# Projections on TensorE: the three products of a tile for two PSUM banks in turn

## What is computed

```python
def first_block(x, ...):
    h = rmsnorm(x, norm_mix_g)
    rq, rk, rv, rg, dq, dk, dv = split(h @ w_in)          # seven projections of 512 columns
    ret = silu(rg) * rmsnorm(retention(rq, rk, rv))        # 4 heads
    dif = rmsnorm(diff_attention(dq, dk, dv, lam)) * ...   # 4 heads, two softmaxes each
    x = x + concat(ret, dif) @ w_out
    xn = rmsnorm(x, norm_ffn_g)
    return rmsnorm(x + peer(xn, wq, subkeys, u, v))        # 16384 one-neuron experts, top 16 of 8 heads

def second_block(x, ...):
    h = rms_norm(x, norm_g)
    q, k, v, qi, ki, wi, z_a, u_b, z_b, gates = split(h @ w_in_2)
    a = dsa_attention(q, k, v, qi, ki, wi, k_sel) * silu(z_a)   # index scores choose 128 keys
    b = multiscale_pool(u_b, ...) * silu(z_b)
    g = sigmoid(gates + merge_bias)
    y = g[0] * (a @ w_branch_a) + g[1] * (b @ w_branch_b)
    return x + y @ w_out_2
```

## Time and profile before

| | |
|---|---|
| median of 3 executions | 1982.58 us (1982.3 to 1982.94) |
| profiled execution, first to last instruction (span) | 1979.5 us |
| median less the span (start and end around it) | 3.1 us |
| granted TensorE clock, mean | 1.000 |
| PE busy | 1954.4 us, 99% |
| DVE, ACT, POOL busy | 1212.9, 728.8, 875.7 us |

### The profile page before, as it was taken

The page is one execution under the profiler, slowest core; times in us unless marked ns, Lnnn a source line. Parts: engine busy times, 40 slices in busy tenths (PEclk is TensorE's granted clock), DMA queues, the critical chain, the costliest instruction groups (busy, mean ns, idle before and its releaser), DMA issues.

```text
span 1979.5 us, 23758 instructions
## 1 busy us (share of the span) xinstructions
PE 1954.4 (99%) x9127; PEld 1586.5 (80%) x9127; DVE 1212.9 (61%) x2188; ACT 728.8 (37%) x1057; POOL 875.7 (44%) x595
## 2 busy tenths in 40 slices
PE   8999999999999999999999999999999999999999
PEld 6777888888888766888888878888888888787787
DVE  3455442499999774222223588888888874795344
ACT  4345432232333344222223333333333334635452
POOL 1000000006878888887700677777787600720000
DMA  7543333146666667866657799999999923332122
GB/s 245 169 136 121 124 111 127 43 142 146 147 147 144 139 118 199 244 146 146 148 183 253 249 373 355 381 373 349 363 375 359 387 75 96 86 88 62 44 95 85
DMA packets 178592, 374.91 MB, mean 189 GB/s; under 512 B 56880, under 2 KB 92208, under 8 KB 169008
## 3 DMA queue, kind: packets, MB, share of 16 engines
q1 hardware_dynamic: 109264, 277.03, 41.0%
q0 software_dynamic: 64000, 84.12, 16.5%
q10 hardware_dynamic: 5216, 12.26, 1.7%
HBM read 312.38 MB, written 60.95 MB: 189 GB/s over the span
## 4 chain that ended last, share of the span: by engine, by line
PE 95%; DVE 3%; ACT 1%; issue 1%; DMA 0%; SPq 0%; DVEq 0%; ACTq 0%
PE bank L1558 35%; PE bank L329 18%; PE bank L331 17%; PE bank L330 17%; PE bank L1438 1%; PE bank L2237 1%; PE bank L1184 1%; PE bank L2217 1%; PE bank L548 1%; PE bank L2226 1%; PE bank L569 0%; DVE mix L919 0%; PE bank L419 0%; DVE v_low L1813 0%; PE bank L604 0%
## 5 line engine op out<-in xcount | busy, mean ns | idle before, releaser
L1412 POOL DMA_INDIRECT gates_scratch<-slot_gate,slot_place x256 | 441.5, 1725 | 299.4 <-DVE slot_place L1379 205.6
L1558 PE MATMUL bank<-xn_low,u_high 128*128 128x512 f32 x1024 | 410.3, 401 | 0.0
L1558 PE MATMUL bank<-xn_high,u_high 128*128 128x512 f32 x1024 | 399.9, 391 | 0.0
L1558 PE MATMUL bank<-xn_high,u_low 128*128 128x512 f32 x1024 | 398.6, 389 | 0.0
L1609 DVE TENSOR_TENSOR u_low<-u_raw,u_high 128x1024 fp32r<-128x1024 f32 x128 | 156.4, 1223 | 265.1 <-ACT u_high L1580 264.7
L329 PE MATMUL bank<-v_high,w_high 128*128 128x512 f32 x768 | 299.3, 390 | 1.4 <-DVE v_low L1813 1.4
L330 PE MATMUL bank<-v_low,w_high 128*128 128x512 f32 x768 | 299.1, 390 | 0.0
L331 PE MATMUL bank<-v_high,w_low 128*128 128x512 f32 x768 | 299.1, 389 | 0.0
L322 DVE TENSOR_TENSOR weights_low<-weights_raw,weights_high 128x1024 fp32r<-128x1024 f32 (+1 forms) x105 | 127.7, 1217 | 228.2 <-ACT weights_high L311 228.2
L1704 POOL DMA_INDIRECT row_unit<-units_scratch,slot_place x128 | 175.1, 1368 | 145.8 <-DMA units_scratch<-hidden 107.1
L1697 POOL DMA_INDIRECT row<-in_peer_v,row_places x128 | 188.7, 1474 | 82.4 <-DVE x L1824 48.9
(11 more groups left out here) (344 smaller groups left out, 3046.7 us busy)
## 6 DMA issues: line engine op xcount, KB each, us to landing
u_raw<-in_peer_u SPq DMA_DIRECT2D x128, 512.0 KB, 4.1
v_raw<-in_peer_v SPq DMA_DIRECT2D x64, 1024.0 KB, 7.6
weights_raw<-in_w_in SPq DMA_DIRECT2D x62, 512.0 KB, 3.6
hidden_scratch<-hidden SPq DMA_DIRECT2D x128, 192.0 KB
hidden_in<-hidden_scratch SPq DMA_DIRECT2D x32, 768.0 KB, 11.7
gates_scratch<-nothing POOLq DMA_DIRECT2D x32, 512.0 KB, 2.9
gate_in<-gates_scratch SPq DMA_DIRECT2D x32, 512.0 KB, 7.3
weights_raw<-in_w_out SPq DMA_DIRECT2D x16, 512.0 KB, 3.7
```

The lines of the kernel that those rows point to most:

```text
L1412: pool.engine.indirect_dma_start(gates, bass.IndirectOffsetOnAxis(p.slot_place[t][:, i:i + 1], 0), p.slot_gate[t][:, i:i + 1], None, compu ...
L1558: step = pe.engine.matmul(m.bank[b][:, :], left[:, k, :], right[:, k, :], start=(done == 0), stop=(done == 3 * KT - 1))
```

## The change

A new helper issues the first product for two banks, then the second for both, then the third for both. `project_tensor` takes the banks in pairs: it waits for both to be empty, goes over the chunk's tiles with both, signals `multiplied` twice, on the last matmul of either bank, and calls `between()` twice behind the pair. The programs of ACT and DVE are the same as before.

```diff
--- before.py
+++ after.py
@@ -331,6 +331,15 @@
     return engine.matmul(out, ll, rh, start=False, stop=last)
 
 
+def two_banks(engine, items, first, last):
+
+    for out, (lh, ll), (rh, rl) in items:
+        engine.matmul(out, lh, rh, start=first, stop=False)
+    for out, (lh, ll), (rh, rl) in items:
+        engine.matmul(out, lh, rl, start=False, stop=False)
+    return [engine.matmul(out, ll, rh, start=False, stop=last) for out, (lh, ll), (rh, rl) in items]
+
+
 def project_tensor(m, name, data, data_ready, banks, freed, between=None):
 
     st, pe, s = m.stream, m.pe, m.s
@@ -339,25 +348,32 @@
     for c in range(g.chunk, g.end):
         weight_high, weight_low = st.part(st.high[c % st.PAIRS], c), st.part(st.low[c % st.PAIRS], c)
         pe.wait_ge(s.weights_low, c + 1)
-        for i, b in enumerate(banks):
+        for first_bank in range(0, len(banks), 2):
+            two = [(i, banks[i]) for i in range(first_bank, first_bank + 2)]
             if c == g.chunk:
-                m.await_bank(b)
+                for i, b in two:
+                    m.await_bank(b)
             for r in range(g.rows):
                 k = (c - g.chunk) * g.rows + r
-                if i == 0:
+                if first_bank == 0:
                     pe.wait_ge(*data_ready(k))
-                part = slice(i * P, i * P + P if g.token_major else min(i * P + P, g.width))
-                if g.token_major:
-                    left = (high[:, k, part], low[:, k, part])
-                    right = (weight_high[:, r, 0:g.width], weight_low[:, r, 0:g.width])
-                    out = m.bank[b][:, 0:g.width]
-                else:
-                    left = (weight_high[:, r, part], weight_low[:, r, part])
-                    right = (high[:, k, :], low[:, k, :])
-                    out = m.bank[b][0:part.stop - part.start, :]
-                done = three_products(pe.engine, out, left, right, k == 0, k == g.tiles - 1)
-            done.then_inc(s.multiplied, 1)
+                items = []
+                for i, b in two:
+                    part = slice(i * P, i * P + P if g.token_major else min(i * P + P, g.width))
+                    if g.token_major:
+                        left = (high[:, k, part], low[:, k, part])
+                        right = (weight_high[:, r, 0:g.width], weight_low[:, r, 0:g.width])
+                        out = m.bank[b][:, 0:g.width]
+                    else:
+                        left = (weight_high[:, r, part], weight_low[:, r, part])
+                        right = (high[:, k, :], low[:, k, :])
+                        out = m.bank[b][0:part.stop - part.start, :]
+                    items.append((out, left, right))
+                done = two_banks(pe.engine, items, k == 0, k == g.tiles - 1)
+            for step in done:
+                step.then_inc(s.multiplied, 1)
             if between is not None:
+                between()
                 between()
     for i, b in enumerate(banks):
         m.bank_freed[b] = freed(i)
```

## The result

| | before | after |
|---|---|---|
| median | 1982.44 us (1980.76 to 1982.94, 4 executions) | 1996.05 us (1994.42 to 1998.2, 4 executions) |
| ratio | | 1.0072, 95% interval 1.0060 to 1.0084 |
| profiled execution, own time / span | 1980.76 / 1979.5 us | 1998.2 / 1996.9 us |
| granted clock, mean of the execution | 1.000 | 0.995 |

The kernel is slower by 0.7%, 13.6 us. That lies above the forecast of 1986.3 us and above its range. The two profiled executions stand further apart than the medians, 17.4 us: the one of before is the fastest of its four and the one of after the slowest.

What follows compares the result with a forecast made beforehand. TensorE was taken to bound the kernel, busy 1954.4 of 1979.5 us. Losses of 7.8 less gains of 3.9 gave +3.9, taken as +3.7 on 1982.58: 1986.3 us, range 1981.5 to 1990.5.

Steps and rivals of the forecast that it cites:

- item 4: Second block's attention (gate01, gate10, start of gate11): merged transposes and multiplies wait on ACT's copies; 3.2 lost, 1.4 gained, +1.8 us.
- The rival that the lost cover costs much more: Each of 12 pairs of merged pieces stalls about 1 us; 1995 us, or 1989 for half; chance 0.22.
- Rate: Projection matmuls: alternating banks gains nothing, 227 ns either way; wq0 to wq3 should still take 86.5 us.
- the rival of faster alternation: Projections: a fixed 11 ns a matmul is a same-bank cost that falls away, 28 us; 1958 us; chance 0.05.
- Two completion signals: Rival, 210 pairs of bank ends: signals on neighbouring matmuls cost time, 2 us at 0.01 us each; 1988 us; chance 0.05.
- Item 1: ret_gate: ACT and DVE chain starts one bank later and the third score waits about 2.3 us; +1.35 us.
- Item 2: End of w_out1: bank 2 is done later, delaying DVE's scales that PE already waits for; +1.13 us.
- Item 3: Index scores in u_b: cover before ACT's relus goes (+0.5) and later evictions delay the third set (+0.9); +1.4 us.
- Item 5: Tail: DVE's add of bank 3 waits behind the later add of bank 2; +0.4 us.
- Item 6: Start of kv: six matmuls a tile instead of three no longer outrun DVE's h_low; -0.85 us.
- Item 7: w_out0: the 0.74 us wait for DVE's 16 scalings is covered by the bank now before it; -0.7 us.
- Item 8: Small ones: two last-bank evictions queue behind a neighbour's, +0.3 us; 30 fewer passages between pieces and projections, -0.9 us.

Runs made afterwards that it cites:

- experiment 3: Kernel before with banks paired only in projections that have no pieces in between (48 of 106 chunks); 1983.28 us, ratio 1.0005.
- experiment 4: Kernel before, bank by bank, with pieces of banks 0 and 2 held back behind banks 1 and 3 in gate00 to gate11 only; 1986.55 us, ratio 1.0025.
- experiment 7: Kernel after with a piece between a pair's two tiles, but each projection's last chunk bank by bank again; 1982.01 us, ratio 1.0000.
- experiment 8: Kernel before; first chunks of diff_q and kv: banks 0/1 tile by tile, bank 1 awaited separately; one piece held back in w_out0 and gate10; 1980.18 us.
- Experiments 2: Kernel before, bank by bank, with pieces of banks 0 and 2 held back behind banks 1 and 3 everywhere, no alternation; 1993.25 us, ratio 1.0054.
- experiment 5: Kernel before, bank by bank, with pieces of banks 0 and 2 held back behind banks 1 and 3 in ret_gate alone; 1985.83 us, ratio 1.0022.
- experiment 1: Kernel after, still alternating, but a pair's first piece goes between its two tiles and its second behind the pair; 1991.69 us, ratio 1.0051.
- experiment 9: Like experiment 4, but ACT copies an item's turned weights before the exp of the next item; 1988.85 us, ratio 1.0035.

## Why the prediction was wrong

The direction of the likeliest case was right, its size was not: +3.7 us forecast, +13.6 us measured. Three steps failed: item 4, the attention, was put at +1.8 us and measured +5.4; the wait for two banks at once was put at nothing and costs 1.3 us; and TensorE's clock had no term, where it takes 6.8 us of the 17.4 between the profiled executions. The rival that the lost cover costs much more (1989 to 1995 us) came nearest, and its far end falls short of the median by 1 us. The mechanisms that it had and missed, step by step:

- **Rate: right.** 0.227 us a matmul in wq after, shifts of 9.02 us at all four starts, and experiment 3 at 1.0005. With it falls the rival of faster alternation.
- **Two completion signals: nothing.** By the rule of the Trainium skill (TensorE: Matmul & The Clock Gate, section The cost: per-tile semaphore tail) the 32 pairs of wq would cost, as an estimate, 32 x 26.3 ns = 0.84 us; the ledger has 0.00. Between ends that are a matmul apart nothing of it shows.
- **Item 1, ret_gate: the wait right, the clock missed.** +1.2 us of waits (1.35 forecast; third score 2.03 us, "about 2.3" forecast), and 2.6 us more since PE ran at 1.2 GHz around it.
- **Item 2, w_out1: right.** +1.14 against +1.13 us; 1.7 us in the wait.
- **Item 3, index scores: the wait right.** +1.3 us of waits against +1.4; then 1.5 us of a spell at 1.2 GHz.
- **Item 4, attention: the term that was mis-sized most.** +5.4 us against +1.8. The losses are 5.9 us against 3.2, and the gain 0.5 against 1.4. I priced a merged pair at 0.2 to 0.5 us, from ACT's copy of 0.25 us and an eviction ahead of it. The round that loses its cover is the longer one, score, DVE, exp, copy, of 3.3 us (experiment 4). The wait of 1.00 us did go, and gained 0.54 us. The transposes waited 6.5 us where I had said some 3; the threshold of 6 us that I had set for the stage was itself too high to show the error.
- **Item 5, tail: right.** +0.5 against +0.4 (0.69 - 0.23 is 0.46, which I had rounded down).
- **Item 6, kv: half missed.** -0.8 us came, as forecast, but +0.6 us stand ahead of it: the pair awaits both banks. The change says so in its text, and I priced nothing for it. The same step costs diff_q +0.7. Both show in experiments 3 and 7, and are gone in experiment 8.
- **Item 7, w_out0: right, and short by its twin.** -1.0 against -0.7, but +0.6 at its start, where ACT's evictions of ret_gate end later. Experiments 2 and 5 have the same 0.6 with no bank ending late, so it belongs to the merged pieces; pairs with spread pieces (experiment 1) lose 0.3 there.
- **Item 8, small ones.** The gain of 0.9 us for 30 fewer passages does not exist: where pieces were merged and no wait changed (ret_k) the steps sum to 0.0. A merged pair in ret_v cost 0.9 us (the wait of 0.6 at L585), which I had under +0.3.
- **The clock, no term at all.** 6.8 us of the 17.4 in the profiled pair of executions. I had read the mean of 1.000 and not asked whether PE's stretches of small pieces and waits would get a lower clock if they grew. The Trainium skill (TensorE: Matmul & The Clock Gate, section HAM oscillation — how this bites in real kernels) takes half of the time at half clock as the penalty. By it the spells of 6.8, 6.8 and 3.4 us would cost an estimated 8.5 us. The trace has less, 6.8 or 5.0 us by the two ways of dividing, and PE stood idle in parts of them (it was busy for 5.13 us of the second).
- **The base.** I carried 3.1 us between span and median over. In fact it is 1.3 us of start and end (1980.76 - 1979.5). The rest fits one spell of 3.4 us, which the profiled execution did not have and about half of the executions of before seem to, by their clock. That did not move the forecast.

In sum the forecast's +3.7 us of waits should have been 10.7: 3.6 from item 4, 1.3 from the awaited banks, 0.9 from ret_v, 0.9 from the passages, 0.3 from w_out0 (+0.6 against 0.3 more gained). These make the 7.0 that are missing; what else is off by 0.1 or 0.2 us nearly cancels. The medians are 13.6 us apart, so some 2.9 us of that are the clock's.

What the runs show for these causes: late ends of banks are shown by experiment 7 against 1, merged pieces by 2, 4 and 5, the awaited banks by 3 and 7 against 8. That it is the whole round which lacks cover in item 4 is read from the traces of experiment 4 and of before; experiment 9 excludes only the order of the copy. The first two causes overlap: in the last chunks the pieces of a pair are late both ways, so merging alone costs 11 us and pairs with spread pieces 9 us, but together 13.6. Why the clock falls at these three places and not at others stays open: I only know what stands there (fp32 pieces of attention, retention or index scores, and a wait of about 2 us), that it comes and goes between executions at 88 us, that of the twelve profiled executions only the three with a wait of 2.0 us in ret_gate show it near 200 us, and that only the three with a wait of 1.9 us or more for relu show it at 1685 us.

## What to carry to other kernels

Changing the order of matmuls within a stream that was already dense gained nothing here, so the price of the reordering was all in what moved with it: when each bank ends, what the pair waits for, and where the interleaved pieces now stand. Price a held-back piece not by the instruction that stands next to it, but by the whole round through the other engines that its cover used to hide, and follow the end of each bank into the queue of the engine that evicts it. Where the new order is better in a few places (here in three of 106 chunks), take these alone: experiment 8 gained 2.1 us with the reordering that lost 13.6 us when it was applied everywhere.

## What was not expected of the hardware

A clock of 1.2 GHz appears in the midst of a kernel whose PE is 98% busy, for 3.4 or 6.8 us at a time, beside waits of no more than 2.3 us. At 88 us it is there in some executions and not in others of kernels that are the same up to that point: experiments 4 and 9 have it, experiment 5 and the kernel before do not. Such a spell of 3.4 us moves the time by 1.5 to 1.6 us. The two groups of execution times of the kernel before, near 1980.8 us (mean clock 1.000) and 1982.4 us (0.999), lie just that far apart; that the second group has its spell at 88 us is not shown, as no execution of it was profiled. A difference of 1 to 2 us between two kernels should be read group by group.
